# Weight granules multiplied once in float32 out of four load buffers, in place of three float32r products of split halves

## The reference

```python
for l in range(DEPTH):                                     # DEPTH = 2, D_MODEL = 1024, D_FF = 2816
    x = layer_norm(ALPHA * x + 0.5 * swiglu(x, ffn1_w_in[l], ffn1_w_out[l]), ln1_g[l], ln1_b[l])
    proj = x @ w_in[l]                                     # 1024 -> 2696 columns
    # three mixers over slices of proj: RWKV-7, sliding-window attention, gated DeltaNet
    mix = concatenate([y_rwkv, y_attn, y_gdn], -1) @ w_out[l]       # 1024 -> 1024
    x = layer_norm(ALPHA * x + mix, ln2_g[l], ln2_b[l])
    x = layer_norm(ALPHA * x + 0.5 * swiglu(x, ffn2_w_in[l], ffn2_w_out[l]), ln3_g[l], ln3_b[l])
```

## Time and profile before

| | us |
|---|---|
| median of three runs | 3039.74 |
| the profiled execution | 3037.87 |
| its span, first to last instruction | 3036.1 |
| TensorE (PE) matmul busy in the span | 2744.6 |
| VectorE (DVE) busy | 1652.3 |
| ScalarE (ACT) busy | 941.4 |
| GpSimd (POOL) busy | 179.6 |

### The profile page before, as it was taken

How to read it: one execution, slowest core, us unless ns; L and a number is a source line. 1 busy time by engine, 2 the same in 40 slices (tenths; PEclk the granted TensorE clock), 3 DMA queues, 4 the chain that set the end, 5 groups by cost and what they waited for, 6 DMA issues and landing times.

```text
span 3036.1 us, 59313 instructions
## 1 busy us (share of the span) xinstructions
PE 2744.6 (90%) x23248; PEld 2565.4 (84%) x23248; DVE 1652.3 (54%) x2489; ACT 941.4 (31%) x1679; POOL 179.6 (6%) x186
## 2 busy tenths in 40 slices
PE   8999999978787799999999999998887688999995
PEld 8999998856565699999999999987665567999994
DVE  5666346745555356663366643565555543666533
ACT  4333233322212133332233332343222212433322
POOL 1030110000000020001100001000000002000010
PEclk9999999977676699999999999998686768999997
DMA  4842334200000223232222222421000012223221
GB/s 110 99 90 87 88 114 113 56 8 1 9 9 5 72 77 90 83 90 85 84 79 88 85 86 87 130 91 32 5 9 1 9 38 80 77 83 90 86 85 47
DMA packets 381441, 201.60 MB, mean 66 GB/s; under 512 B 41381, under 2 KB 378789, under 8 KB 380472
## 3 DMA queue, kind: packets, MB, share of 16 engines
q1 hardware_dynamic: 378872, 197.46, 22.6%
q0 software_dynamic: 2400, 1.82, 1.8%
HBM read 188.07 MB, written 13.34 MB: 66 GB/s over the span
## 4 chain that ended last, share of the span: by engine, by line
PE 80%; DVE 10%; issue 5%; ACT 4%; SPq 1%; DMA 0%; DVEq 0%; ACTq 0%; POOLq 0%; POOL 0%
PE ps L656 55%; PE ps L710 22%; DVE ar L1805 3%; DVE ar L1799 2%; ACT ar L1336 2%; SPq L517 1%; PE ps L1059 1%; PE ps L964 1%; ACT wh L1267 1%; DVE wl L1683 1%; DVE x L1713 0%; DVE x L1799 0%; DVE ar L1835 0%; DVE x L1711 0%; DVE xl L1790 0%
## 5 line engine op out<-in xcount | busy, mean ns | idle before, releaser
L1683 DVE TENSOR_TENSOR wl<-raws,wh 128x1024 fp32r<-128x1024 f32 x332 | 406.5, 1225 | 734.5 <-ACT wh L1267 730.5
L656 PE MATMUL ps<-xh,wh 128*128 128x272 f32 x3136 | 662.7, 293 | 43.8 <-DVE xl L1799 18.2
L656 PE MATMUL ps<-xh,wl 128*128 128x272 f32 x3136 | 656.3, 291 | 0.0
L656 PE MATMUL ps<-xl,wh 128*128 128x272 f32 x3136 | 654.8, 290 | 0.0
L710 PE MATMUL ps<-ar 64*64 64x64 f32 (+13 forms) x4984 | 495.3, 294 | 122.8 <-ACT ar L1336 38.2
L710 PEld LDWEIGHTS ps<-ar 64*64 64x64 f32 (+5 forms) x4984 | 370.1, 179 | 223.4 <-issue 64.0
L656 PEld LDWEIGHTS ps<-xh,wh 128*128 128x128 f32 x3136 | 502.1, 192 | 49.7 <-issue 26.5
L656 PEld LDWEIGHTS ps<-xl,wh 128*128 128x128 f32 x3136 | 502.0, 191 | 0.0
L656 PEld LDWEIGHTS ps<-xh,wl 128*128 128x128 f32 x3136 | 501.1, 191 | 0.0
L1267 ACT ACTIVATE wh<-raws 128x1024 fp32r<-128x1024 f32 x332 | 350.6, 1057 | 455.9 <-PE ps L656 430.6
L656 PE MATMUL ps<-hh,wh 128*128 128x272 f32 x1408 | 292.2, 289 | 0.0
(11 more groups left out here) (188 smaller groups left out, 2755.2 us busy)
## 6 DMA issues: line engine op xcount, KB each, us to landing
raws<-in_ffn_w_in SPq DMA_DIRECT2D x176, 512.0 KB, 3.7
raws<-in_ffn_w_out SPq DMA_DIRECT2D x64, 512.0 KB, 4.0
raws<-in_w_in SPq DMA_DIRECT2D x42, 512.0 KB, 3.6
raws<-in_ffn_w_out SPq DMA_DIRECT2D x32, 384.0 KB, 3.4
raws<-in_w_out SPq DMA_DIRECT2D x16, 512.0 KB, 4.1
x_kept<-x SPq DMA_DIRECT2D x2, 2176.0 KB, 10.2
x<-x_kept SPq DMA_DIRECT2D x2, 2176.0 KB, 7.9
ar<-in_consts SPq DMA_DIRECT2D x2, 1337.5 KB, 6.5
```

Source lines behind the costliest of these rows:

```text
L656: ins = pe.matmul(ps[:, bank + h, 0:n1 - h * NH], w[u % 2][:, k, :], a[:, k0 + k, h * NH:n1], start=(first and k == 0 and n == 0), stop=(l ...
L1683: dve.tensor_tensor(wl[u % 2][:, :, :], raw[u % 2][:, :, :], wh[u % 2][:, :, :].bitcast(F32), ALU.subtract).then_inc(sem("wl_done"), 1)
```

## The change

The float32r copies go: `xl`, `wh`, `wl` and `hl` are no longer there, and `xh`, `hh` and the raw weights are plain float32. PE multiplies each block once, straight out of the load buffer, and waits for the load's own semaphore. There are four load buffers in place of two, each free when PE has ended its granule. In `granule` all blocks for the first half of the columns come first, then all blocks for the second half; `proj_part` keeps both halves inside the loop over blocks. `split` is gone on ACT and DVE, and `x_low_part`, `z_low` and DVE's `g_cols` with it; DVE writes the hidden values and the head pairs' outputs straight into `hh` and `xh`. `keep_busy` is gone. The first two granules of the output product are loaded at the end of the projection. The counting of buffers goes up by two places after the projection's 22 granules.

```diff
-        xh = sb("xh", [P, KC, NX], F32R)
-        xl = sb("xl", [P, KC, NX], F32R)
-        raws = sb("raws", [P, 2, 8, P])
-        wh = [... F32R for s in range(2)]
-        wl = [... F32R for s in range(2)]
+        xh = sb("xh", [P, KC, NX])
+        raws = sb("raws", [P, SLOTS, 8, P])          # SLOTS = 4
...
             def load(lay, g, u, src):
-                sp.wait_ge(sem("wl_done"), at(lay, "wl_done", g + u - 1))
-                sp.dma_start(raw[u % 2][...], src).then_inc(raw_in[u % 2], 16)
+                slot = u % SLOTS
+                sp.wait_ge(sem("mm_done"), at(lay, "mm_done", g + u - SLOTS + 1))
+                sp.dma_start(raw[slot][...], src).then_inc(raw_in[slot], 16)
...
-            def granule(lay, g, u, nblocks, hi, lo, k0, bank, first, last, split_from=None):
-                pe.wait_ge(sem("wl_done"), at(lay, "wl_done", g + u + 1))
-                for k in range(nblocks):
-                    if split_from is not None:
-                        pe.wait_ge(sem("xl_done"), at(lay, "xl_done", split_from + k + 1))
-                    for n, (w, a) in enumerate(((wh, hi), (wh, lo), (wl, hi))):
-                        for h in range(2):
-                            n1 = a.shape[2] if h else NH
-                            ins = pe.matmul(ps[:, bank + h, 0:n1 - h * NH], w[u % 2][:, k, :], a[:, k0 + k, h * NH:n1],
-                                            start=(first and k == 0 and n == 0), stop=(last and k == nblocks - 1 and n == 2))
+            def granule(lay, base, n, u, nblocks, a, k0, bank, first, last, split_from=None):
+                slot = u % SLOTS
+                pe.wait_ge(raw_in[slot], (lay * slot_uses(NG, slot) + slot_uses(base, slot) + n + u // SLOTS + 1) * 16)
+                for h in range(2):
+                    n1 = a.shape[2] if h else NH
+                    for k in range(nblocks):
+                        if split_from is not None and h == 0:
+                            pe.wait_ge(sem("xh_done"), at(lay, "xh_done", split_from + k + 1))
+                        ins = pe.matmul(ps[:, bank + h, 0:n1 - h * NH], raw[slot][:, k, :], a[:, k0 + k, h * NH:n1],
+                                        start=(first and k == 0), stop=(last and k == nblocks - 1))
...
-                        for n, (w, a) in enumerate(((wh, xh), (wh, xl), (wl, xh))):      # proj_part
-                            for h in range(2):
-                                ins = mm(...)
+                        for h in range(2):
+                            n1 = NX if h else NH
+                            ins = mm(ps[:, 2 * u + h, 0:n1 - h * NH], raw[g % SLOTS][:, k, :], xh[:, k, h * NH:n1],
+                                     start=(k == 0), stop=(k == KC - 1))
...
-                            keep_busy(p, 3)              # three places in recurrence, q == 3 only
-                    keep_busy(p, 8)                      # head_norm, q == 3 only
...
-                act.activation(wh[u % 2][:, :, :], raw[u % 2][:, :, :], ACT.Copy).then_inc(sem("wh_done"), 1)
-                act.activation(chunk(hh, i * 2 + u), work[:, 2 + u, :], ACT.Copy).then_inc(sem("hh_done"), 1)
-                    go(xh[:, (q if q < 2 else 4 + q), 0:NT], U[:, TMP, :]).then_inc(*tick("head_h"))
...
-                dve.tensor_tensor(wl[u % 2][:, :, :], raw[u % 2][:, :, :], wh[u % 2][:, :, :].bitcast(F32),
-                                  ALU.subtract).then_inc(sem("wl_done"), 1)
-                tt(xl[:, 2:6, 0:SEQ], y_attn[:, :, 0:SEQ], xh[:, 2:6, 0:SEQ].bitcast(F32), ALU.subtract)
-                        tt(y, y, U[:, GATE, :], ALU.mult).then_inc(*tick("y_final"))
-                    tt(xl[:, ch, 0:NT], y, xh[:, ch, 0:NT].bitcast(F32), ALU.subtract).then_inc(*tick("head_l"))
+                        tt(final, y, U[:, GATE, :], ALU.mult).then_inc(*tick("head_l"))    # final = xh[:, ch, 0:NT]
...
+                for u in range(2):                       # SP, right behind the projection's loads
+                    load(lay, BASE_WO, u, columns(w_mix, lay, (0, KC), u * P))
```

More of the change, by code:

```diff
@@ L46 @@
 N_FFN_IN, N_FFN_OUT = 2 * FC, 3 * KC
+SLOTS = 4
+SKIP = -PC % SLOTS
 BASE_F1I = 0
@@ L53, with slot_uses @@
 NG = BASE_F2O + N_FFN_OUT
+assert all(b % SLOTS == 0 for b in (BASE_F1O, BASE_PJ, BASE_WO, BASE_F2I, BASE_F2O, NG))
+def slot_uses(base, slot):
+    return base // SLOTS - (base >= BASE_WO and slot >= SLOTS - SKIP)
 LAST_ROW = P - 1
@@ L488, in ffn_weights @@
             def ffn_weights(lay, n, base):
[L489 to L493, removed]
+                with sp.Fori(0, FC // 2) as i:
+                    for u in range(4):
+                        load(lay, base + i * 4, u, columns(w_ffn_in[n], lay, (0, KC), i * (2 * P) + u // 2 * P + u % 2 * D_FF))
+                with sp.Fori(0, KC // 4) as d:
+                    for u in range(12):
                         b0 = sum(G_OUT_BLOCKS[:u % 3])
-                        load(lay, base + N_FFN_IN + d * 6, u,
-                             columns(w_ffn_out[n], lay, (b0, b0 + G_OUT_BLOCKS[u % 3]), d * (2 * P) + u // 3 * P))
+                        load(lay, base + N_FFN_IN + d * 12, u,
+                             columns(w_ffn_out[n], lay, (b0, b0 + G_OUT_BLOCKS[u % 3]), d * (4 * P) + u // 3 * P))
             def one_layer(lay):
@@ L611, in one_layer @@
                         put(out("p_" + name, lay)[:, 0, 2 * c + hp, :, :].rearrange("a m n -> (a m) n"), src, "state_out")
-                with sp.Fori(1, KC // 2) as c:
-                    for u in range(2):
-                        load(lay, BASE_WO + c * 2, u, columns(w_mix, lay, (0, KC), c * (2 * P) + u * P))
+                for u in range(4, KC):
+                    load(lay, BASE_WO, u, columns(w_mix, lay, (0, KC), u * P))
+                    sp.sem_inc(passed, 1)
                 ffn_weights(lay, 1, BASE_F2I)
@@ L1053, in inverse @@
                     yield
[L1055 to L1059, removed]
                 def recurrence(p):
@@ L1303, in ffn @@
                 g_cols(lay, 2 * ph, lay + (LN_SLOT[1] if ph == 0 else 1))
-                def out_pair(d, tail):
-                    for u in range(6):
-                        if not (tail and u >= 4):
-                            split(lay, base + N_FFN_IN + d * 6, u + 2)
-                        if u % 3 == 2:
-                            squares(lay, 2 * ph, d * 2, u // 3)
-                            z_high(lay, 2 * ph, lay + (LN_SLOT[1] if ph == 0 else 1), d * 2 + u // 3)
-                with act.Fori(0, KC // 2 - 1) as d:
-                    out_pair(d, False)
-                out_pair(KC // 2 - 1, last)
+                with act.Fori(0, KC // 2) as d:
+                    for u in range(2):
+                        squares(lay, 2 * ph, d * 2, u)
+                        z_high(lay, 2 * ph, lay + (LN_SLOT[1] if ph == 0 else 1), d * 2 + u)
             def g_cols(lay, n, slot):
                 act.wait_ge(sem("lnp_in"), 16 * LN_DMAS)
-                act.activation(xh[:, :, NT:NX], affine_cols(slot), ACT.Copy).then_inc(sem("cols_h"), 1)
+                act.activation(xh[:, :, NT:NX], affine_cols(slot), ACT.Copy)
             def squares(lay, n, c, u):
@@ L1763, in ffn @@
                         pair(i, u)
-                g_cols(lay, 2 * ph, lay + (LN_SLOT[1] if ph == 0 else 1))
-                def out_pair(d, tail):
-                    for u in range(6):
-                        if not (tail and u >= 4):
-                            split(lay, base + N_FFN_IN + d * 6, u + 2)
-                        if u % 3 == 2:
-                            residual(lay, 2 * ph, d * 2, u // 3, base + N_FFN_IN + d * 6 + u + 1, 2 * ph)
-                            z_low(lay, 2 * ph, lay + (LN_SLOT[1] if ph == 0 else 1), d * 2 + u // 3)
-                with dve.Fori(0, KC // 2 - 1) as d:
-                    out_pair(d, False)
-                out_pair(KC // 2 - 1, last)
-            def g_cols(lay, n, slot):
-                dve.wait_ge(sem("cols_h"), at(lay, "cols_h", n + 1))
-                dve.tensor_tensor(xl[:, :, NT:NX], affine_cols(slot), xh[:, :, NT:NX].bitcast(F32), ALU.subtract)
+                with dve.Fori(0, KC // 2) as d:
+                    for u in range(2):
+                        residual(lay, 2 * ph, d * 2, u, base + N_FFN_IN + d * 6 + 3 * u + 3, 2 * ph)
             def residual(lay, n, c, u, g, m):
```

185 lines of the change are left out of this document (56 added, 129 removed).

## The result

The changed kernel took 3387.4 us (median of four runs, 3377.63 to 3388.93) against 3036.35 us for the kernel before (3028.84 to 3040.9). The ratio is 1.1152, 95% interval 1.1119 to 1.1185. The profiled execution of the changed kernel has a span of 3375.7 us, 339.6 us more than the 3036.1 of before.

The account below looks back on a forecast made before the run. The prediction took TensorE's own time per product to bound the feed-forwards, with VectorE and ScalarE mattering only where TensorE waits. It summed 3037.9 + 409 for products - 60 for stalls = 3387 us, range 3340 to 3430 eight times in ten.

Parts of the forecast that it names:

- The product: All 5184 products: one float32 matmul takes 457.8 ns where three float32r matmuls take 378.9, costing +409 us.
- Rival A: Products: a float32 pass costs as much as a float32r matmul in a long stream, 505 ns a product; 3633 us, chance 0.05.
- rival D: Products: a float32 record is worth one pass in a stream, 228 ns a product; 2195 us or more, chance 0.02.
- The stalls: TensorE's waits at boundaries, projection and head pairs, with the filler: -60 us in sum, bounds -30 and -95.
- Start: Kernel start: TensorE begins at 18.95 though the bias row's copy, its last wait, ends at 16.69; -2 us.
- Layer step: Layer 1 to 2: the 6.85 us wait for split weights and the slow 48 matmuls after it go; -9 us.
- Output product to feed-forward: First granule after the output product, still paced by ScalarE's eight copies: 2.8 us saved, twice, -6 us.
- Projection: Waits of 7.5 and 4.3 us lose the split and hide in longer granules: 11 us a layer, -22 us.
- B: Rival: stalls stay because longer granules move every hand-over, only start and layer step gain; 3436 us, chance 0.06.
- Pairs' ends: Each head pair's end: the copy-to-low-part chain of about 1.5 to 1.74 us goes, eight times; -12 us.
- filler: `keep_busy` matmuls on the chain, which hold no clock, are removed: 4.4 us, twice, -9 us.
- Loads at zero: Weight loads and matmul order cost nothing with four buffers; without that cover a granule would pay up to 3.7 us.

Follow-up runs that it names:

- E1: Kernel before with one float32 matmul of the high parts for three float32r ones, splits, buffers and filler kept: 3417.15 us, ratio 1.124.
- E5: Changed kernel with the halves of the columns back inside the loop over blocks in `granule`: 3380.54 us, ratio 1.1107 to the kernel before.
- E2: Kernel before with only the matmul order changed, halves outside the blocks in `granule`, still three float32r matmuls a product: 3057.48 us, ratio 1.0042.
- E6: Changed kernel with weight loads held back until the granule two before is done: 3404.7 us, ratio 1.1198 to the kernel before.
- E7: Changed kernel with feed-forward weight loads held back until the granule before is done: 5087.17 us, ratio 1.6717 to the kernel before.
- E3: Kernel before without its 41 filler matmuls a layer in the last head pair (`keep_busy` off): 3033.78 us, ratio 0.9976.

## Why the prediction was right

The forecast was 3387 us and the measured median 3387.4. That close a hit is luck: the product's term was 8 us too small and the stalls' 18 too small, which cancel to 10 in the profiled execution (3377.6 us), and that execution happens to lie 10 us under its median. The mechanism, that TensorE's time per product decides and the engines beside it don't, was right. The term that was mis-sized is the projection's.

**The product.** Forecast +409 us from 457.8 ns, measured +417 from 459.4. The eight records of the layer norm's sums carried over to 2112 in a row within 0.4%; E1 and E5 give 460.1. Rival A (505 ns) and rival D (228 ns) are out: the 13 ns of float32r aren't in a float32 pass. Four passes a product fit the time, at 114.8 ns a pass. The Trainium skill ("TensorE: Matmul & The Clock Gate", Back-to-back issue gap) gives, as the gap of an isolated matmul, its columns over 2.4 GHz plus 2.5 ns, by an estimate 115.8 ns for 272 columns. The float32 pass lies 1 ns under that and float32r's matmul 10 above it. The change of bank doesn't make up that difference (E2), nor does how often weights come twice in a row: 4 of 6 matmuls in the order of before, 1 of 3 in E2, at the same pace. Two slips in the working: the sign "483 us in place of 382" sets 1056 products against the 1008 of the earlier trace rows (1056 took 400), and the +603 is 601 by the figures beside it; neither enters the sum.

**The stalls.** Forecast -60, measured -78 in the profiled execution. By steps:
- Start, forecast -2: measured +0.6. The bias row's copy was the last wait, as the step had it, and itself came 2 us later, at 18.72; 1.2 of that is the sample tokens' load, which landed later. Other launches started at 17.2 and 18.1 (E6, E5), and those with the split between 18.9 and 20.6.
- Layer step, -9: measured 6.2 + 3.2 = 9.4, and 0 in E1, where the split stays.
- Output product to feed-forward, -6: measured -4.5.
- Projection, -22: measured -40. This is the step that was mis-sized, and its reason was mostly wrong. I named the longer granules too, but gave a figure for the removed split alone, and held it against B. E1 keeps the split and gets 31 of the 40: a longer granule hides the same chain. In the stage's rows TensorE is idle for 17.2 us before, 6.5 in E1 and 2.7 after. The rest of the change adds 9; how much of that is the split and how much the four buffers isn't shown, since E6, without the split but with loads two ahead, loses 13 in the projections. I had counted the waits alone, 11.8 us a layer, where the stage also had a granted clock of 0.97, and 1.00 in E1 and after. B, which had the waits move with the longer granules, is refuted by the same stage.
- Pairs' ends -12 and filler -9, together -21: measured 8.3 + 10.0 = 18 in a stage that scatters by as much, and E1, with nothing changed in it, has 9 of them. The sign holds over the traces: 427.7 to 437.7 us in the kernel before and E2, 411.8 to 421.7 in the changed kernel, E5, E6 and E7. E3 puts the filler at 6, with 9 inside its interval.

**Loads at zero.** Right with four buffers. What stands without the cover is 4.2 us a granule plus a fallen clock (E7), not the "up to 3.7" of the forecast; with loads two ahead it's 17 us in all by the medians, in the first feed-forward and the projections (E6).

## What to carry to other kernels

Three float32r matmuls on split halves beat one plain float32 matmul of the same shape, 379 to 459 ns, where TensorE is the bound and the splitting fits beside it. Removing the splitting gave back less than the 30 us that all of the rest gave, against a price of 417. To price a matmul in another type, look for the smallest place in the same trace that already uses it, count its records per matmul, and measure from start to start. When the bound engine gets slower, the waits in its mixed stages shrink by themselves, so try the slower engine alone before giving the credit to the chain that was shortened.

## What the runs showed of the hardware

- A float32 matmul of 128x128 by 128x272 is two records 229.7 ns apart at full clock in streams of 2112, and 230.0 with the other order of blocks and halves (E5). Float32r's is one record and 126.3 ns, 13 ns above what its columns take at 2.4 GHz. The change of bank isn't in those 13 ns (E2), and their cause stays open.
- Filler matmuls that kept TensorE 23.55 of 25 us busy ran at a granted clock of 0.50, the same as without them at 16.90 of 25 (E3). They brought the next stage's first 48 matmuls from 8.52 to 8.16 us.
- Gaps of some 4.1 us, each behind a granule of 9.0 to 10.6 us, cost the clock only in part: 0.83 granted on the mean (E7).
